# Weight loads in halves among cache copies, with eight-run copy pieces at both ends of each middle stage

## What is computed

```python
u = rms_norm(h, g_norm).reshape(n, d)
gates = route(u, wgr, bgr, wer, ber)         # best group, then its two best experts
a = jnp.einsum('td,edf->tef', ub, wg)        # gate: 1024 -> 512
c = jnp.einsum('td,edf->tef', ub, wu)        # up:   1024 -> 512
hh = jax.nn.silu(a) * c * gb[:, :, None]
out = jnp.einsum('tef,efd->td', hh, wd)      # down: 512 -> 1024
```

## Time and profile before

| | us |
|---|---|
| median of 3 runs | 1184.7 (1181.23 to 1186.34) |
| time of the profiled execution | 1177.72 |
| its span, first to last instruction | 1175.9 |
| PE busy | 1079.4 (92% of the span) |
| DVE busy | 434.1 |
| ACT busy | 216.2 |
| POOL busy | 240.0 |
| moved by DMA | 462.66 MB, mean 393 GB/s |

### The profile page before, as it was taken

The page is one execution under the profiler, slowest core; times in us unless marked ns, Lnnn a source line. Parts: engine busy times, 40 slices in busy tenths (PEclk is TensorE's granted clock), DMA queues, the critical chain, the costliest instruction groups (busy, mean ns, idle before and its releaser), DMA issues.

```text
span 1175.9 us, 14097 instructions
## 1 busy us (share of the span) xinstructions
PE 1079.4 (92%) x4939; PEld 650.8 (55%) x4939; DVE 434.1 (37%) x843; ACT 216.2 (18%) x532; POOL 240.0 (20%) x504
## 2 busy tenths in 40 slices
PE   7999999999955999969999999997579799999997
PEld 4788888888822888843444434444334344434444
DVE  4456656755921666150122202114741122202113
ACT  2222222122110344031111111112111111111110
POOL 1014212221420131005221122221222221122220
PEclk9999999999966799987999999999769899999999
DMA  9999999999999999999999999999999999999998
GB/s 359 363 383 394 388 388 416 387 391 403 410 336 415 341 348 331 377 370 320 429 427 429 429 428 438 426 421 446 350 328 323 435 425 429 429 433 431 423 439 298
DMA packets 61898, 462.66 MB, mean 393 GB/s; under 512 B 11196, under 2 KB 19148, under 8 KB 46836
## 3 DMA queue, kind: packets, MB, share of 16 engines
q1 hardware_dynamic: 48464, 418.28, 89.2%
q10 hardware_dynamic: 7956, 24.88, 6.3%
q0 software_dynamic: 5424, 18.75, 4.1%
HBM read 454.99 MB, written 183.21 MB: 543 GB/s over the span
## 4 chain that ended last, share of the span: by engine, by line
PE 50%; DMA 15%; DVE 5%; issue 2%; ACT 1%; SPq 0%; ACTq 0%; DVEq 0%
PE bank L1274 23%; DMA ring_lo<-in_w_up_dram 12%; PE bank L1244 8%; PE bank L1298 4%; DMA ring_lo<-in_cache_kv_w_dram 3%; PE bank L1197 2%; PE bank L1156 2%; PE bank L1253 1%; PE bank L1164 1%; PE bank L1176 1%; PE bank L1153 1%; PE bank L1260 1%; PE bank L1129 1%; PE bank L305 1%; PE bank L1171 1%
## 5 line engine op out<-in xcount | busy, mean ns | idle before, releaser
L1274 PE MATMUL bank<-ring_lo,scratch 128*64 128x512 f32 x1024 | 340.8, 599 | 10.7 <-DMA ring_lo<-in_w_up_dram 9.2
L1083 PE MATMUL bank<-uT,ring_lo 128*128 128x264 f32 x1152 | 269.9, 388 | 0.4 <-DVE uT L319 0.4
L1083 PEld LDWEIGHTS bank<-uT,ring_lo 128*128 128x128 f32 x1152 | 214.6, 191 | 38.8 <-DMA ring_lo<-in_w_qkv_dram 1.1
L1274 PE MATMUL bank<-region_a,scratch 128*64 128x512 f32 x512 | 227.9, 598 | 0.0
L1274 PEld LDWEIGHTS bank<-ring_lo,scratch 128*64 128x64 f32 x1024 | 106.5, 138 | 149.9 <-issue 149.5
L1244 PE MATMUL bank<-scratch 128*128 128x512 f32 (+1 forms) x216 | 119.0, 679 | 3.1 <-DVE scratch L956 3.1
L801 DVE RECIPROCAL scratch<-scratch 128x264 f32<-128x264 f32 x48 | 86.5, 1803 | 94.2 <-ACT scratch L639 94.2
L1274 PEld LDWEIGHTS bank<-region_a,scratch 128*64 128x64 f32 x512 | 67.8, 137 | 65.9 <-issue 64.0
L981 DVE TENSOR_TENSOR scratch<-bank,scratch 128x512 f32<-128x512 f32 x16 | 11.1, 692 | 246.5 <-PE bank L1274 246.5
L988 DVE TENSOR_TENSOR hT<-bank,hT 128x264 f32<-128x264 f32 x128 | 55.4, 433 | 119.9 <-PE bank L1298 118.6
L547 POOL TENSOR_TENSOR small<-epsc 128x1 f32<-128x1 f32 x71 | 13.8, 195 | 374.1 <-PE bank L1260 358.2
(11 more groups left out here) (226 smaller groups left out, 1108.7 us busy)
## 6 DMA issues: line engine op xcount, KB each, us to landing
out_dram<-in_cache_kv_w_dram SPq DMA_DIRECT2D x107, 1023.5 KB, 19.8
ring_lo<-in_w_up_dram SPq DMA_DIRECT2D x32, 2048.0 KB, 22.0
ring_lo<-in_w_qkv_dram SPq DMA_DIRECT2D x18, 2048.0 KB, 21.3
ring_lo<-in_w_gate_dram SPq DMA_DIRECT2D x16, 2048.0 KB, 14.3
region_a<-in_w_down_dram SPq DMA_DIRECT2D x16, 2048.0 KB, 15.5
region_a<-in_w_gate_dram SPq DMA_DIRECT2D x16, 2048.0 KB, 19.6
ring_lo<-in_w_down_dram SPq DMA_DIRECT2D x16, 2048.0 KB, 20.0
out_dram<-in_cache_kv_w_dram SPq DMA_DIRECT2D x32, 1022.0 KB, 21.5
```

Of the source, the lines that this page charges most:

```text
L1083: last = mm(z_bank[i % 4][:, 0:T], w[:, k, at:at + P], uT[:, k, :], start=(k == 0), stop=(k == KT - 1))
L1274: last = mm(out[rows, :], lhs[:, k, rows], weights[e][w][:, k, columns], start=(k == 0), stop=(k == k_tiles - 1))
```

## The change

1. Slots have a second semaphore (`ring_half`). The loads of pair 0 (all but their first) and of pair 8 are issued as two halves of 1 MB, in `expert_in_halves` and `first_pair_of_layer_1`, with 0 to 3 pieces behind each half. In the rounds of these pairs PE waits for the first half of a slot, and for the second where its products begin. For pair 8 the halves of both experts alternate. All other loads stay whole.
2. The pieces of ACT's queue move to SP. By the new `COPIES`, 108 pieces go up to the end of the first middle stage, 11 in layer 0 (pairs 1 to 7), 28 with pair 8 and the pooling stage, 11 in layer 1 and 10 behind the last weights.
3. In each middle stage two of these pieces are issued as two transfers of eight runs each: the first eight runs ahead of the halves (`move_first_halves`), the last eight behind them (`move_last_halves`).
4. `keep_busy` adds products to the router on PE whose results are not used: 5 ahead of the wait for the normalized tokens, 8 ahead of the wait for the chosen experts.
5. The pooling products use four banks in place of two, and DVE adds outputs 0 to 3 between the pooling groups and the rest behind them, before it copies the state tokens. ACT's squares of the next norm stand ahead of the state's stores.

```diff
@@ -211,6 +211,7 @@
 z_bank = [bank[n] for n in (0, 1, 6, 7)]
+pool_bank = [bank[n] for n in (1, 2, 5, 6)]
@@ -218,6 +219,7 @@
 ring_full = [sem(f"ring_full{n}") for n in range(6)]
+ring_half = [sem(f"ring_half{n}") for n in range(6)]
 dve_own, pool_own = sem("dve_own"), sem("pool_own")
@@ -274,8 +276,10 @@
-COPIES = {"first_chunks": 7, "chunk": (3, 3, 3), "last_chunks": 3, "sample_half": (2, 0), "head": (1, 2), "heads_end": 3,
-          "router_0": 7, "pair": (((1, 0, 0), (1, 0, 1)), ((1, 0, 1), (1, 0, 1))), "pool": 14}
+COPIES = {"first_chunks": 7, "chunk": (3, 3, 3), "last_chunks": 3, "sample_half": (2, 0), "head": (1, 2), "heads_end": 4,
+          "pair_0_early": (2, 1), "pair_0_late": ((2, 2), (2, 1)), "pair": ((1, 0, 0), (1, 0, 1)),
+          "pair_8": ((1, 1, 1, 2), (2, 2, 2, 2), (3, 3, 3, 1)), "pool": 3}
+IN_HALVES = 4
 ATTN_G, POOL_G, FFN_G, POOL_B, POOL_S = 0, KT, (2 * KT, 3 * KT), 4 * KT, 5 * KT
@@ -349,7 +353,6 @@
 pieces = [(g, b, n) for g in range(G) for b in range(NS) for n in range(PIECES[g])]
-ACT_PIECES = (7, 14)
@@ -367,6 +370,18 @@
             moves_begun.append((g, b, n))
+    def move_first_halves(count):
+        split = pieces[len(moves_begun):len(moves_begun) + count]
+        for g, b, n in split:
+            sp.dma_start(moved[g][0][b, n, 0:8], moved[g][1][b, n, 0:8]).then_inc(cache_copied, 16)
+            moves_begun.append((g, b, n))
+        return split
+    def move_last_halves(split):
+        for g, b, n in split:
+            sp.dma_start(moved[g][0][b, n, 8:16], moved[g][1][b, n, 8:16]).then_inc(cache_copied, 16)
@@ -408,24 +423,33 @@
-    expert(0, 0, 0)
-    move_next(3)
+    def expert_half(e, odd, what, part):
+        s, n = SLOTS[odd][what], (FT if what == 2 else KT) // 2
+        sp.dma_start(slot(s)[:, part * SLOT // 2:(part + 1) * SLOT // 2].rearrange("p (k f) -> p k f", k=n),
+                     expert_w[what][e][:, part * n:(part + 1) * n, :]).then_inc((ring_half, ring_full)[part][s], 16)
+    def expert_in_halves(e, odd, what, copies):
+        for part in range(2):
+            expert_half(e, odd, what, part)
+            move_next(copies[part])
+    expert_in_halves(0, 0, 0, (0, 3))
     for h in range(4, H):
...
     sp.wait_ge(biased, H)
-    expert(0, 0, 1)
+    split = move_first_halves(2)
+    expert_in_halves(0, 0, 1, COPIES["pair_0_early"])
     sp.wait_ge(qk_staged, PAIRS)
     sp.wait_ge(v_staged, PAIRS)
-    expert(0, 0, 2)
-    expert(1, 1, 0)
-    move_next(4)
+    expert_in_halves(1, 1, 0, COPIES["pair_0_early"])
+    expert_in_halves(0, 0, 2, COPIES["pair_0_early"])
     sp.wait_ge(wo_ready, KT)
-    expert(1, 1, 1)
-    expert(1, 1, 2)
-    move_next(COPIES["router_0"])
+    expert_in_halves(1, 1, 1, COPIES["pair_0_late"][0])
+    expert_in_halves(1, 1, 2, COPIES["pair_0_late"][1])
+    move_last_halves(split)
@@ -435,18 +459,30 @@
+    def first_pair_of_layer_1(rounds):
+        for what, used, per in ((0, gates_done, 1), (1, ups_done, 1), (2, y_half, 2)):
+            sp.wait_ge(used, rounds * per)
+            if what == 0:
+                split = move_first_halves(2)
+            for n in range(4):
+                expert_half(NP * 2 + n % 2, n % 2, what, n // 2)
+                move_next(COPIES["pair_8"][what][n])
+        move_last_halves(split)
     def rounds_at(layer, p):
...
     sp.wait_ge(rounds_ready, 1)
-    for p in range(1, NP + 1):
-        next_pair(p, rounds_at(0, p), COPIES["pair"][0][p % 2])
+    for p in range(1, NP):
+        next_pair(p, rounds_at(0, p), COPIES["pair"][p % 2])
+    first_pair_of_layer_1(rounds_at(0, NP))
     move_next(COPIES["pool"])
...
     for p in range(1, NP):
-        next_pair(p + NP, rounds_at(1, p), COPIES["pair"][1][p % 2])
-    move_next(len(pieces) - sum(ACT_PIECES) - len(moves_begun))
+        next_pair(p + NP, rounds_at(1, p), COPIES["pair"][p % 2])
+    move_next(len(pieces) - len(moves_begun))
@@ -455,7 +491,7 @@
     sp.wait_ge(y_sent, 48)
-    sp.wait_ge(cache_copied, 16 * len(pieces))
+    sp.wait_ge(cache_copied, 16 * (len(pieces) + IN_HALVES))
@@ -710,16 +746,12 @@
             norm_root(ac, 2, layer_added, 1, per_k=0)
-            for piece in pieces[len(pieces) - ACT_PIECES[1]:]:
-                move(ac, *piece)
+            norm_root(ac, 3, pool_y_added, 1)
             ac.wait_ge(pool_tok_ready, 1)
...
             dma(pool_s[0, :, STATE - 1, :], pool_tok[STATE:STATE + NS]).then_inc(pool_sent, 16)
-            norm_root(ac, 3, pool_y_added, 1)
         else:
             norm_root(ac, 1, wo_added, 1)
-            for piece in pieces[len(pieces) - sum(ACT_PIECES):len(pieces) - ACT_PIECES[1]]:
-                move(ac, *piece)
         for b in range(3):
@@ -999,6 +1031,13 @@
+    def add_pool_y(first, end):
+        for m in range(first, end):
+            dve.wait_ge(pool_y_ready, m + 1)
+            chain(vec.tensor_scalar(ybuf[:, m % 2, :], pool_bank[m % 4][:, 0:T], vecs[:, POOL_B + m:POOL_B + m + 1],
+                                    vecs[:, POOL_S + m:POOL_S + m + 1], ALU.add, ALU.mult))
+            vec.tensor_tensor(hT[:, m, :], hT[:, m, :], ybuf[:, m % 2, :], ALU.add).then_inc(pool_y_added, 1)
     norm_apply(dve, chain, 2, POOL_G)
@@ -1025,15 +1064,13 @@
         dve.wait_ge(pooled, gi + 1)
+        if 1 <= gi <= 2:
+            add_pool_y(2 * gi - 2, 2 * gi)
+    add_pool_y(4, 8)
     for a in range(2):
...
     last.then_inc(pool_tok_ready, 1)
-    for m in range(KT):
-        dve.wait_ge(pool_y_ready, m + 1)
-        chain(vec.tensor_scalar(ybuf[:, m % 2, :], bank[1 + m % 2][:, 0:T], vecs[:, POOL_B + m:POOL_B + m + 1],
-                                vecs[:, POOL_S + m:POOL_S + m + 1], ALU.add, ALU.mult))
-        vec.tensor_tensor(hT[:, m, :], hT[:, m, :], ybuf[:, m % 2, :], ALU.add).then_inc(pool_y_added, 1)
@@ -1197,8 +1234,14 @@
+    def keep_busy(out, products):
+        for _ in range(products):
+            mm(out, ident[:], ones[:].rearrange("p (a n) -> p a n", a=1).to_broadcast([P, 2, P]), start=True, stop=True)
     def router(layer, n_norm):
         pe.wait_ge(router_landed, 16 * N_ROUTER)
+        keep_busy(bank[5][:, 0:2 * P], 5)
         for k in range(KT):
@@ -1221,6 +1264,7 @@
         pe.wait_ge(tri_landed, 16)
+        keep_busy(bank[6][:, 0:2 * P], 8)
         pe.wait_ge(chosen_ready, layer + 1)
@@ -1262,13 +1306,17 @@
     def one_round(q, p, layer):
-        def weights_there(s):
-            pe.wait_ge(ring_full[s], p * 16 + 16 * (layer * NP + FIRST_USES[s] + 1))
+        def weights_there(s, part):
+            if p == 0 and part == 0:
+                pe.wait_ge(ring_half[s], 16 * (layer + 1))
+            elif (p == 0) == (part == 1):
+                pe.wait_ge(ring_full[s], p * 16 + 16 * (layer * NP + FIRST_USES[s] + 1))
         def both_experts(out, lhs, w, k_tiles, columns):
-            for e in range(2):
-                weights_there(SLOTS[e][w])
             for k in range(k_tiles):
+                if k % (k_tiles // 2) == 0:
+                    for e in range(2):
+                        weights_there(SLOTS[e][w], k // (k_tiles // 2))
                 for e in range(2):
@@ -1336,10 +1384,10 @@
             pe.wait_ge(wide_pooled, 1)
-        if m >= 2:
-            pe.wait_ge(pool_y_added, m - 1)
+        if m >= 4:
+            pe.wait_ge(pool_y_added, m - 3)
         for ct in range(2):
-            last = mm(bank[1 + m % 2][:, 0:T], pw[:, 2 * gi + ct, ft * P:(ft + 1) * P], pool_z[:, 2 * gi + ct, :], start=(ct == 0), stop=(ct == 1))
+            last = mm(pool_bank[m % 4][:, 0:T], pw[:, 2 * gi + ct, ft * P:(ft + 1) * P], pool_z[:, 2 * gi + ct, :], start=(ct == 0), stop=(ct == 1))
         last.then_inc(pool_y_ready, 1)
```

## The result

| | before | after |
|---|---|---|
| median of 4 runs, us | 1184.83 (1181.23 to 1186.34) | 1171.64 (1168.01 to 1175.19) |
| ratio | | 0.9894, 95% interval 0.9872 to 0.9917 |
| the profiled execution, us | 1177.72 | 1171.47 |
| its span, us | 1175.9 | 1169.7 |

The forecast was 1171, made against a median of 1184.7. First the table by stretch of the kernel after, with the stretches of the earlier trace rows; the last three numbers are granted clock, DMA share and GB/s.

The account below looks back on a forecast made before the run. The prediction took transfers to end the kernel, so the sum is of DMA time: -6.1 - 9.6 - 7.3 + 9.7 = -13.3 us, span 1162.6, median 1171 us. The range was 1157 to 1187.

Parts of the forecast that it names:

- First middle stage: Output projection to experts: copies spread among half loads run at 385 GB/s, and a rest is filled: -6.1 us.
- the rest in 460 to 480: First middle stage: engines rested 3 us before SP could pass the last bias; a fourth copy fills that.
- Second middle stage: From 791 to 911 us: copies spread among twelve half loads, one copy fewer, at 385 GB/s: -9.6 us.
- the rival that mixing gives no rate: Both middle stages: copies cost what they did; total -0.5 us, 1184 us, chance 0.14.
- The -20 us: Second middle stage's term if memory gave the skill page's 716 GB/s, with copies counted twice; not taken.
- Layer 1 and the tail: Three copies leave layer 1's weights, -7.3 us, and come back alone behind the last weights, +9.7 us.
- The split pieces: Both middle stages: half pieces of eight runs load different engines, bytes being equal: 0 us.
- the same-eight rival: Split pieces' halves load the same eight engines: +9.8 us before the last weights land, net +5, 1176 us; chance 0.24.
- the sign that the prediction had named: Layer 0: PE waits of several us on L1274 would speak for split pieces loading the same eight engines.
- PE's parts: Both middle stages: held clock saves PE 10 and 8.6 us, pool outputs 5.4; hidden by transfers, so 0.
- the 1.5 added to it: Pool outputs, second middle stage: estimated 1.5 us more, as the norm's sums no longer queue behind L1342.
- Issue: ACT's 21 issues and some thirty more of about 0.5 us go to SP, hidden in its 469 us of waits.

Follow-up runs that it names:

- seven_last: The changed kernel with the pair counts of layer 1 all (1, 0, 1), so seven and not ten copies end it: 1172.83 us, ratio 0.9881.
- after_again: The changed kernel itself, measured once more: 1166.66 us, ratio 0.9876.
- clumped_sp_inputs: As clumped, but with the seven loads of the pooling's inputs issued by SP behind the first pair's weights: ratio 1.0034.
- whole_loads_sp_inputs: As whole_loads, but with the seven loads of the pooling's inputs issued by SP behind the first pair's weights: ratio 0.9941.
- whole_pieces: The changed kernel with its four split pieces undone, one whole piece copied at each place: 1173.1 us, ratio 0.9914.
- no_pe_parts: The changed kernel without keep_busy and with the pool outputs in two banks and behind the state's copy again: 1170.82 us, ratio 0.9935.
- the pair with late inputs: The changed kernel with the pooling's inputs loaded one behind each of pairs 1 to 7: 0.9957; the same with seven copies at the end: 0.9936.
- whole_loads: The changed kernel with the weights of pairs 0 and 8 loaded whole, both halves' copies behind each load: 1183.79 us, ratio 1.0040.
- clumped: The changed kernel with pair 0's remaining and pair 8's weights loaded whole, ahead of all copies of their group: 1193.11 us, ratio 1.0109.

## Why the prediction was right

**What bounds it.** The kernel ended when its transfers did, before and after: PE's last round was done 16.7 us ahead of the end, and SP waited 8.5 us for copies when all else was stored.

**First middle stage**, predicted -6.1, measured -5.2, -3.1 and, in seven_last, whose code is the same here, -1.0: a mean of -3.1, half of the forecast. The rate in 500 to 560 was no worse than taken (396 and, in after_again, 377 against 385), the rest in 460 to 480 filled less than taken (.85 to .94). What limits the stage now is no longer the rate: DMA share in 540 to 560 is .96, and .84 in after_again, because bytes run out before PE asks for more. That the stage would come to PE's side was not in the prediction. The prediction also overlooked a hole in the kernel before, which the change fills. SP waited for the output projection until 502.5, its queue was nearly empty, and 492 to 502 moved 206 GB/s, where the changed kernel moved 400 in 484 to 520:

```profile
DMA packets 1479, 2.06 MB, mean 206 GB/s; under 512 B 193, under 2 KB 1380, under 8 KB 1472
...
q10 hardware_dynamic: 1449, 1.60, 60.2%
q1 hardware_dynamic: 30, 0.46, 11.8%
```

So part of what this stage gained is bytes where there were none, and not a better rate; the runs do not part the two.

**Second middle stage**, predicted -9.6, measured -10.5, -10.0 and -9.2: 391 GB/s against the 385 taken, so the rival that mixing gives no rate (363) is out. This is the spreading: with the weights whole and ahead of all copies B to C is 352.8 or, with the inputs on SP, 349.8; with whole loads spread among the copies 344.9, and with halves 343.7. Halving the loads is thus worth about 1 us here beyond spreading them, which is no more than the stage's own scatter. That the copies of ACT's queue now go from SP did nothing by itself: clumped_sp_inputs, with all on SP, has 349.8 us, one copy's 3.2 us under the 353.1 before, and it has one copy less there. Between clumped_sp_inputs and whole_loads_sp_inputs, which differ in the place of the copies and in the order of two loads of pair 0, the whole time differs by 0.9% (1.0034 to 0.9941), some 11 us, of which the ledger shows 7.1. The -20 us that the figure of the Trainium skill (HBM Reference, Specifications) would have given did not come.

**Layer 1 and the tail**, predicted -7.3 and +9.7, measured -7.2 and +10.3 (after_again +9.2). The mechanism and both prices held. Ten copies behind the last weights took 33.9 us, 3.39 each, where 3.22 was taken from a stretch of copies alone. The seven_last kernels undo both terms with the sign turned.

**The split pieces**, predicted 0, the same-eight rival at 0.24. Refuted: the trace has 128 packets of 32752 B, which whole_pieces has not: 16 for each of the eight transfers, its runs cut in two. I had supposed one run to an engine. The instruction that was issued has sixteen elements of 32752 B. The trace names no engine, so that sixteen engines carried them is an inference; but layer 0 has no wait for a load, the sign that the prediction had named, and the kernel with the halves was not slower than the one without. The Trainium skill (DMA: Bandwidth & Descriptors, "Why a DMA increments its semaphore by 16 and not by 1") lets the slowest dimension as the instruction carries it decide, and adds that software may split a contiguous pattern to reach sixteen; I weighed the first of these and not the second.

**PE's parts**, predicted 0, as transfers hide them. In the ledger it nearly held: no_pe_parts is within 2.6 us from A to E. Its ratio is 0.4 to 0.6% above the change's, which no stage of the ledger explains, so what they are worth to the whole time, 0 or some 5 us, stays open. The sizes that were under the 0 were off. From the first sums of the norm to the experts it took 39.7 us before and in no_pe_parts, and 33.8 after, so 5.9 and not 10; in the second stage 40.9, 38.7 and 34.3, so 4.4 to 6.6 and not 8.6. And the 5.9 is one execution's: with the same code it took 37.9 us in after_again and in seven_last, a gain of 1.8. The first gather of after_again, beside the 7.41 us above:

```profile
528.49 10.47 PE bank L1288 x12
```

The granted clock in 526 to 538 was 0.86 after, 0.51 in after_again and 0.68 in seven_last, 0.50 before. In the first stage the products of `keep_busy` thus held the clock in one of three executions; in the second in all three (gathers of 7.48, 7.46 and 7.44 us against 11.51). It fell later there, and the gates and ups took 16.42 and 16.20 where before they took 15.22 and 13.91. A to B of the three is 189.7 us where the first gather took 7.41, and 191.8 and 193.9 where it took 10.5, and the pair with late inputs goes the same way (188.0 with 7.58, 190.4 with 10.42). So a part of PE's time may count in this stage, against the price of 0; it is not shown, as whole_pieces has 196.3 with a gather of 7.50. The new order and banks of the pooling outputs gave 3.9 us (from sums to sums 35.2 to 31.3), exactly the difference worked out, without the 1.5 added to it. Experts of layer 1 began at 877.7 and not near 863, so PE waited 3.9 us for the up weights, not some 10.

**Issue**, predicted as hidden. For SP's added issues that held: all it took away is time in which SP waits for the experts' products (469.3 us before at L409, 444.2 after: 432.1 at L424, 12.1 at two other lines). Some 0.5 us each was right for copies (ACT issued seven in 4.8 us before), but it is no rule: the seven loads of the inputs, which the change left alone and the prediction did not weigh, held ACT 26 us before and 28 after, in the path of the norm. In the changed kernel ACT came free 1.3 us before the residual was complete. That this cost nothing was luck, not part of the prediction, and only the experiments that lengthened it brought it out.

So the mechanism was right, and three of the four terms of the sum by their own steps: -13.3 us forecast, -12.6 and -11.1 in the ledgers of two executions, and 12.6 and 14.6 us by the two ratios. The fourth, the first middle stage's, is -3.1 in the mean of three and not -6.1. That the total lies so near is in part chance, as the ledgers' scatter of 2 us a stage is as large as what is missing.

## What to carry to other kernels

Where transfers bound a kernel and some of them are memory-to-memory copies, spread these among the loads: here the second middle stage went at 391 GB/s instead of 363. It was the place of the copies that counted; the size of the loads mattered, as far as the runs show, only through how long ACT stood at its own small loads. In this kernel small loads went nearly free between large packets of another queue, in a stage whose queue had room for them. Where they had the engines alone they moved at 232 GB/s, and spread through the expert layer, whose queue was full already, they went with a loss of more than their bytes' time, whose cause the runs do not part. Before moving a transfer, ask which engine stands at its issue, and what is behind that issue in the engine's order.

## What the runs showed that I had not expected

- **An issue can hold its engine for tens of microseconds.** ACT stood 26 us before and 28 us after at seven loads of 2.08 MB together, 42 in whole_loads, 44 in clumped; SP stood 38 us at four of them.
- **Two queues share the engines packet by packet.** 314 packets of 1 KB went beside 316 of 24 KB in the mean, 997 beside 998 of 13 KB.
- **A transfer of eight runs of 64 KB is sixteen packets** of 32752 B here, as many as a transfer of sixteen runs has.
- **The clock's fall was only put off, and not each time.** Granted clock in 526 to 538 went from .50 to .86, but 0.5 showed in 540.9 to 547.8 during the first gates; what the products saved in the gather (4.1 us) was partly paid there (1.2 us). In after_again and seven_last, with the same products, the first gather took 10.5 us, and the first gates were slow too (16.4 us in after_again).
- **A packet of a copy costs by its company**: 2.4 us in the mean among the weights of layer 0, 2.5 to 2.7 in the middle stages after, 3.0 to 3.1 in the same stages before (2.8 and 3.2 in 840 to 890).
